# Dealing the next group's dots between the stages on VectorE, with gelu behind ScalarE's stages

## The reference, cut to what matters

```
h  = rmsnorm(x) @ w_in                        # latents, rotary keys, conv inputs
o  = softmax(q_lat.ckv + q_rope.kr) ckv       # 4 heads, causal; the 8 samples read paged caches of 2048 keys
x1 = x + [group_rmsnorm(attn), group_rmsnorm(conv)] @ w_o
q  = rmsnorm(x1) @ w_query                    # 8 heads x 2 x 128
sv, si = top_k(q . sub_keys, 16)              # per half
experts, g = top 16 of the 16 x 16 sums, softmax of their scores     # 8 x 16 = 128 slots a token
a  = gelu(x . expert_u[experts])
x2 = x1 + sum over the 128 slots of (g * a) * expert_v[experts]
y  = rmsnorm(x2)
```

## Time and profile before

| what | value |
|---|---|
| median of 3 runs | 3510.18 us (3496.6 to 3515.45) |
| the profiled execution | 3510.76 us, its span 3509.0 us |
| busy share of the span | PE 72%, DVE 65%, POOL 66%, ACT 23% |
| mean granted clock of TensorE | 0.839 of full speed |
| moved by DMA | 1279.45 MB |
| its queues' share of 16 engines | gathers (POOL's) 80.6%, SP's 12.5%, ACT's 2.3% |

### The profile page before, as it was taken

One profiled execution on the slowest core, in us unless ns is written; L12 is line 12 of the kernel. 1 busy time (PEld: TensorE's weight loads), 2 busy tenths in 40 slices (PEclk: granted clock), 3 DMA queues, 4 the chain that ended last, 5 costly groups with the idle time before them and its releaser, 6 DMA issues.

```text
span 3509.0 us, 38717 instructions
## 1 busy us (share of the span) xinstructions
PE 2510.7 (72%) x11488; PEld 1386.8 (40%) x11488; DVE 2278.5 (65%) x5454; ACT 813.6 (23%) x2057; POOL 2300.2 (66%) x2068
## 2 busy tenths in 40 slices
PE   7558775878764598877644977778546888875755
PEld 6426443545531264445311643345213534332421
DVE  3685586655688756657898466558796454544874
ACT  2112212232212212322112123322113122222111
POOL 0466575755657777676777767667777585657774
PEclk9779887999986799898876999889777798988776
DMA  6699899988999999999999999899999999999997
GB/s 237 241 389 375 329 410 333 392 306 302 372 346 373 373 402 372 353 369 412 408 359 375 405 385 355 329 376 409 400 368 374 379 388 359 371 334 398 411 409 305
DMA packets 368935, 1279.45 MB, mean 365 GB/s; under 512 B 59372, under 2 KB 77974, under 8 KB 353368
## 3 DMA queue, kind: packets, MB, share of 16 engines
q0 software_dynamic: 297216, 1082.26, 80.6%
q1 hardware_dynamic: 62324, 168.67, 12.5%
q10 hardware_dynamic: 9188, 26.05, 2.3%
HBM read 1262.31 MB, written 13.48 MB: 364 GB/s over the span
## 4 chain that ended last, share of the span: by engine, by line
DVE 37%; PE 31%; DMA 15%; issue 7%; ACT 4%; SPq 3%; POOL 2%; DVEq 0%; ACTq 0%; POOLq 0%
DVE u_ring L1736 15%; PE acc L924 9%; DMA u_ring<-in_expert_u,pick_cur 8%; PE front L586 8%; PE front L802 3%; DMA v_ring<-in_expert_v,pick_cur 3%; DVE si_u L1603 2%; SPq L536 2%; DVE sv L1602 2%; PE front L711 2%; DMA w_ukT<-in_cache_krope 2%; DVE work L1603 2%; DVE work L1602 1%; DVE work L1647 1%; DVE work L1649 1%
## 5 line engine op out<-in xcount | busy, mean ns | idle before, releaser
L924 PE MATMUL acc<-v_ring,diag 128*64 128x512 f32 x4096 | 1176.0, 723 | 614.6 <-ACT diag L1222 344.4
L1851 POOL DMA_INDIRECT v_ring<-in_expert_v,pick_cur x1024 | 1146.5, 1120 | 607.3 <-PE acc L924 334.3
L1851 POOL DMA_INDIRECT u_ring<-in_expert_u,pick_cur x1024 | 1136.9, 1110 | 569.1 <-issue 292.3
L1736 DVE CUSTOM_DVE_ANT_0 u_ring<-u_ring,xn_cur 128x1024 f32<-128x1024 f32 x1024 | 1209.9, 1222 | 335.1 <-DMA u_ring<-in_expert_u,pick_cur 329.4
L924 PEld LDWEIGHTS acc<-v_ring,diag 128*64 128x64 f32 x4096 | 342.6, 164 | 1331.4 <-issue 878.5
L1222 ACT ACTIVATE diag<-ident,wgt 128x64 f32<-128x64 f32 x1024 | 272.8, 338 | 787.1 <-DVE wgt L1742 734.9
L586 PE MATMUL front<-work,w_ring 128*128 128x256 f32 (+2 forms) x1536 | 306.4, 341 | 31.8 <-DVE mo L1337 17.1
L586 PE MATMUL front<-mo,w_ring 128*128 128x256 f32 (+2 forms) x1536 | 298.2, 335 | 0.0
L1215 ACT ACTIVATE gelu<-dots 128x4 f32<-128x4 f32 x256 | 52.7, 206 | 996.5 <-DVE dots L1736 992.8
L586 PEld LDWEIGHTS front<-work,w_ring 128*128 128x128 f32 x1536 | 249.0, 199 | 83.9 <-issue 28.6
L586 PEld LDWEIGHTS front<-mo,w_ring 128*128 128x128 f32 x1536 | 252.0, 198 | 23.9
(11 more groups left out here) (303 smaller groups left out, 2375.7 us busy)
## 6 DMA issues: line engine op xcount, KB each, us to landing
w_ring<-in_w_pieces SPq DMA_DIRECT2D x112, 1024.0 KB, 8.4
u_ring<-in_expert_u,pick_cur POOLq DMA_INDIRECT x1024, 10.5
v_ring<-in_expert_v,pick_cur POOLq DMA_INDIRECT x1024, 9.9
x_t<-in_x_prompt SPq DMA_DIRECT2D x16, 512.0 KB
v_ring<-in_w_pieces SPq DMA_DIRECT2D x8, 1024.0 KB, 12.0
work<-in_cache_ckv SPq DMA_DIRECT2D x64, 128.0 KB, 15.2
xn_cur<-scratch ACTq DMA_DIRECT2D x14, 512.0 KB, 9.7
scratch_x<-rows_next ACTq DMA_DIRECT2D x8, 512.0 KB, 6.8
```

The costliest lines, as they stand in the source:

```text
L924: last = nc.tensor.matmul(acc[rows, half, :], diag[:, s % RING, :], v_ring[:, s % RING, half * 512:half * 512 + 512], start=(s < 2), stop= ...
L1736: v.tensor_tensor_reduce(u_ring[:, slot, :], u_ring[:, slot, :], xn2_cur[:, block_of(r), :], 1.0, 0.0, ALU.mult, ALU.add, dots[:, g * G + ...
L1851: pool.indirect_dma_start(ring[:, slot, :], None, a[table][0], bass.IndirectOffsetOnAxis(ap=pick, axis=0)).then_inc(loaded[slot], 16)
```

## The change

On DVE the dots of g+1 are cut in shares: one share stands at the head of the group, ahead of the weighing of g, and one behind each stage. With no stage or one the shares are 2 and 2; with two stages 2, 1, 1; with three 1, 1, 1, 1. On ACT gelu of g+1 (and the load of the next tile's tokens) always stands behind the stages. PE, POOL and SP keep their order, and the special cases for `pages` go.

```diff
+def shares(n, k):
+    cuts = [(n * i + k) // (k + 1) for i in range(k + 2)]
+    return list(zip(cuts[:-1], cuts[1:]))
...
             def tile(it):                                   # ScalarE
                 for g, stages in enumerate(PLAN[it]):
-                    late = has_pages(stages)
                     if g:
                         diag_group(it, g)
-                    if g and not late and g + 1 < GROUPS:
-                        gelu_group(it, g + 1)
-                    if g == GROUPS - 2 and not late and it < LAST:
-                        load_xn2(it + 1)
                     for s in stages:
                         stage(own, *s)
-                    if g and late and g + 1 < GROUPS:
+                    if g and g + 1 < GROUPS:
                         gelu_group(it, g + 1)
-                    if g == GROUPS - 2 and late and it < LAST:
+                    if g == GROUPS - 2 and it < LAST:
                         load_xn2(it + 1)
...
             def tile(it):                                   # VectorE
                 for g, stages in enumerate(PLAN[it]):
-                    half = G // 2 if has_pages(stages) else G
+                    dots_due = g > 0 and g + 1 < GROUPS
+                    parts = shares(G, max(1, len(stages)))
+                    if dots_due:
+                        dot_group(it, g + 1, *parts[0])
                     if g:
                         weigh_group(it, g)
-                    if g and g + 1 < GROUPS:
-                        dot_group(it, g + 1, 0, half)
-                    ahead = 1 if has_pages(stages) else len(stages)
-                    for s in stages[:ahead]:
-                        stage(own, *s)
-                    if g and g + 1 < GROUPS:
-                        dot_group(it, g + 1, half, G)
-                    for s in stages[ahead:]:
-                        stage(own, *s)
+                    for n, part in enumerate(parts[1:]):
+                        if n < len(stages):
+                            stage(own, *stages[n])
+                        if dots_due:
+                            dot_group(it, g + 1, *part)
```

## The result

The changed kernel takes 3563.82 us (median of 5, 3561.53 to 3565.84) against 3503.06 us (median of 5, 3496.6 to 3515.45): ratio 1.0162, 95% interval 1.0146 to 1.0179, so slower by 57 us (the two medians lie 61 us apart). The profiled execution took 3563.91 us, its span 3562.1 us at a mean clock of 0.843; before it was 0.839, so the clock is no part of the loss. The forecast was 3531 us: its sign holds, its size is a third of the loss.

The account below looks back on a forecast made before the run. No single engine bounds the program; it alternates. Terms +13 +10 +5 +8 -10 -5 +4 -5 sum to +20 us on 3510.8: forecast 3531 us, own range 3518 to 3555, whole range 3482 to 3580.

Parts of the forecast that it names:

- Term 1: One-stage query groups: MAX8 waits for the scores' copy behind ACT's diags, 0.87 us more each; +13 us, ends 0 and +21.
- Term 2: Groups without stages behind a long DVE stage: a late weigh holds PE's v_group; +10 us, and +5 behind a `select`.
- Term 3: Selects and long stages: POOL stops at the third u gather; ends 0 and 126 us, taken +8 at three tops stretches.
- Term 4: Multi-stage groups: a dot fills each DVE wait between stages; ends 0 and -26 us, taken -10.
- Term 5: gelu behind ACT's stages: weigh's wait for it goes under dots, -5 us; Exp and Ln tables load behind diag, +4.
- A: Rival, whole kernel: the DMA sets the pace, no change; 3505 to 3518 us, say 3512; chance 0.30.
- B: Rival, multi-stage groups: faster, all 23 holes pay; -32 us, 3479 us; chance 0.24.
- C: Rival: clearly slower, POOL stands at the third u through every select and long stage; 3565, at worst about 3600 us; chance 0.12.

Follow-up runs that it names:

- e14: The changed kernel with the weighing ahead of the dots only in the 40 groups whose one stage is a query: 1.0081 of the kernel before.
- e7: The changed kernel with ACT copying the scores ahead of the diags in groups that begin with a query: 1.0176 of the kernel before, second occasion.
- e1: The kernel before with the ACT part of the change alone, gelu behind ACT's stages, DVE's order as before: 0.9978 of the kernel before.
- e10: The changed kernel with the weighing ahead of the dots only in the 29 groups without a stage: 1.0168 of the kernel before.
- e11: The changed kernel with the weighing ahead only in groups whose one stage is no query: 1.0136 of the kernel before.
- e6b: The changed kernel with POOL's order fitted to the dot shares in tiles 1 to 5 alone, fourth occasion: 1.0164 of the kernel before.
- e13: The changed kernel with the weighing ahead of the first share and POOL's order fitted in tiles 1 to 5: 1.0013 of the kernel before.
- e3b: The changed kernel with the weighing ahead of the first share in all groups, fourth occasion: 1.0021 of the kernel before.
- e6: The changed kernel with POOL's order fitted to the dot shares in tiles 1 to 5 alone, second occasion: 1.0157 of the kernel before.
- e9: The kernel before with gelu behind ACT's stages and the scores' copy ahead of the diags, VectorE as before: 0.9935 of the kernel before.
- e4: The kernel before with the changed order only in groups with two or three stages: 1.0013 of the kernel before.
- e12: Same as e9, with dots dealt out in groups of two and three stages behind a weighing that stays ahead: 0.9921 of the kernel before.
- e0: The changed kernel unedited, run again on the second occasion as the mark: 1.0251 of the kernel before.
- e5: The kernel before with only the weighing moved behind the four dots: 1.0256 of the kernel before, second occasion.

## Why the forecast was right in sign and wrong in size

The change is slower for the reason that the forecast gave first, a weighing that comes too late. Two steps failed. The late weighing (terms 1 and 2) was taken at +28 us, and putting it ahead gives 49. And the load of the next tile's tokens, which the change moves with gelu and which waits for the tile's last dots, had no term at all: the tile ends where it is waited for cost 26 us.

**Term 1 (MAX8 behind the diags): right.** Its 0.87 us per group is 0.85 in the row (0.60 to 1.45). The one-stage query groups add 20 us in sum, against +13 taken and an end of +21. Leaving nine groups out, because they run into waits for u rows, was the error in it: tiles 3, 5 and 7 give 13.5 of the 20, and tiles 0 and 1 only 6.6. In tile 1 the weighings of two neighbouring query groups lie 12.42 us apart before (mean of that tile) and 13.29 now, 0.87 more. e14 and e7 show the path. What the forecast had not seen is that the ACT part alone *removes* part of the 0.60 us, since gelu no longer waits for the last dot ahead of the copy: the MAX8 line waits 52.6 us in e1 and 57.1 in e14, against 77.3 in the kernel before. The late weighing takes this gain away too, which fits that moving it forward gives 28 us and not 13 to 21.

**Term 2 (a late weigh holds PE's v_group): the mechanism stands, its place and price failed.** Behind mix_norm, in the changed kernel, DVE and PE:

```profile
1527.29 1.23 DVE L1569 TENSOR_TENSOR work<-work,vec_cols 128x1024 f32<-128x1024 f32 x1
```
```profile
1532.89 5.54 PE L930 MATMUL acc<-v_ring,diag 128*64 128x512 f32 x16 [10.80 <-ACT diag L1228]
```

From the start of mix_norm's last operation to the v_group it is 5.60 us. Before, that operation, which stood just ahead of the earlier trace rows, was

```profile
1518.88 1.23 DVE L1568 TENSOR_TENSOR work<-work,vec_cols 128x1024 f32<-128x1024 f32 x1
```

and the v_group followed at 1521.05, 2.17 us behind. The 3.43 us are the forecast's 3.44. But e10, which puts the weighing back in all 29 groups without a stage, shortens that stretch:

```profile
1531.82 1.23 DVE L1569 TENSOR_TENSOR work<-work,vec_cols 128x1024 f32<-128x1024 f32 x1
...
1534.46 0.16 DVE L1743 TENSOR_TENSOR wgt<-gelu,gate_cur 128x4 f32<-128x4 f32 x1 [0.27 <-ACT gelu L1221]
```
```profile
1535.49 5.10 PE L930 MATMUL acc<-v_ring,diag 128*64 128x512 f32 x16 [10.01 <-ACT diag L1228]
```

to 3.67 us, and shows no gain: 1.0168. The +10 and +5 were worth 0, with some 8 us either way left open by the intervals. Meanwhile the forecast gave nothing to one-stage groups other than queries: by the stage matching they lose 13 us, and e11 has 0.26%, 9 us, there, which its interval does not tell from nothing. The weighing ahead everywhere gives 49 us (1.0162 to 1.0021); with 28 in query groups, 9 in other one-stage groups and 0 without a stage, each within some 10 us, some 12 us are left to groups of several stages or to what only shows when all are moved. Terms 1 and 2 together had +28.

**Term 3 (POOL meets a closed door): it costs nothing where it was read, and beside it a term is missing, the tokens' load.** "It costs nothing if the queues hold enough ... and all of it if POOL is full afterwards", and then I took the near end, +8 us at three tops stretches. At the select that I had read it costs nothing, indeed. POOL stops at the third u gather, as forecast, but its idle there is what it was ahead of the first one in the earlier trace rows:

```profile
1112.52 1.18 POOL L1851 DMA_INDIRECT u_ring<-in_expert_u,pick_cur  x1 [5.04 <-DVE dots L1737]
```

With POOL's order fitted nothing comes back on the fourth occasion (e6b, and e13 beside e3b), 0.9% on the second (e6). The cost that no part of the sum holds is at the tile ends, 26 us by the jumps above. The forecast puts ACT's load of the next tile's tokens at nothing by not naming it, though the change moves it. It takes 12.7 to 13.7 us from issue to landing, and at all six ends the first dot starts 0.02 to 0.12 us behind the landing.

The jumps stay in every kernel that splits the dots around a single stage (e3b 24 us, e13 25 us). e9 moves the load behind ACT's stages but has all four dots ahead of them: its jumps are 8 us, and its dots still wait for the tokens in tiles 0, 2 and 4 (7.06, 2.30 and 12.47 us). So some 8 us belong to ACT's order and the rest, 18, to the late share. Over e1, where the kernel before was at its longer level, e4 has -3, e12 3, e0 10 and e6 17 us, but e5 has 11 without any late share, so there something else adds to them. No kernel moved the load by itself, and what an earlier one would give back was not measured.

**Term 4 (a dot in each hole): right where it was read, nothing in sum.** Between two heads of tile 1 the dot stands where the wait for the transposes was the earlier trace rows:

```profile
727.47 0.61 DVE L1494 SCALAR_TENSOR_TENSOR work<-low_keys,small,front 128x384 f32<-128x384 f32 x1 [1.16 <-PE front L718]
...
733.61 0.16 DVE L1743 TENSOR_TENSOR wgt<-gelu,gate_cur 128x4 f32<-128x4 f32 x1
...
735.20 0.61 DVE L1494 SCALAR_TENSOR_TENSOR work<-low_keys,small,front 128x384 f32<-128x384 f32 x1 [0.97 <-PE front L718]
```

The 0.64 us is gone and 1.57 became 1.16; in exchange a wait of 0.97 us for the scores stands behind the front dots. The group has 12.84 us from weighing to weighing (720.77 to 733.61), before 13.39 (721.66 to 735.05): 0.5 us shorter, where the chain of front, PE and v_group was to give near nothing. In tile 1, behind its norms, after lies 9 us before the old kernel, and 5.5 us ahead of its tops; over the whole program the groups of several stages, without the tile ends, come out at -5 us against the -10 taken, and e4, which deals out in these alone, at 1.0013.

**Term 5 (gelu): right on its wait.** Weigh waits for gelu 16 times instead of 80, 22.3 us instead of 33.2. Of these, 8 (6.7 us) stand in the last group of a tile; the longest, 6.4 us, is in tile 1 (weighing at 705.8), where gelu now stands behind ACT's part of three stages. gelu's table is still loaded 80 times and hides. e1's 0.9978 agrees with -5 + 4 within its interval; what it is worth beyond the MAX8 waits was not measured.

**The sum again, by place**, in the two profiled executions (+53 us): query stages +20 (forecast 13), tile ends +26 (no term; the 8 of term 3 stood at the tops), other one-stage groups +13 and groups of several stages -5 (together with the rest +7, forecast -1 without the 8). And by cause, in medians: late weighing +49 (forecast 28); late shares and the rest +7 (forecast -8), in which tile ends of some 25 us (still there in e3b) and the gains elsewhere stand against each other.

**The rivals.** A (the DMA sets the pace) held in part in tile 0, where the DMA is near its limit: the MAX8 waits of its query groups grow by 8.8 us and their stages end 3.5 us later. B's holes pay little. C asked for idle of over 10 us ahead of that u gather; it is 5.04, so C did not happen though the time is near its 3565: the right number by another sum.

## What to carry to other kernels

When operations are rotated in a loop, look first at the small one: a weighing of 0.16 us, moved behind 2.3 us of dots, cost 1.4% of the program, over half of it (0.81%) in the groups where a copy on another engine was queued behind four operations that wait for it. Put what other engines wait for first and the bulk behind it, and let an engine that copies for a waiting one do this copy ahead of work that nobody needs yet (e9: 0.65% in five runs with an interval of 0.4%, gelu's move included). When the last readers of a buffer with one copy move back, the load that refills it moves back too: here DVE's idle time at six tile ends grew with it from 15 to 43 us. A stage by stage difference of two traces shows where time goes when no total of waits does: here POOL's wait for dots grew by 287 us in a kernel that takes 1.0021 of the time (e3b).

## What the runs showed that I had not expected

- The same edit cost 1.6% on one occasion and 2.5% on another. It is not the chip alone: on chip 13 the kernel before took 3609, 3607 and then 3505 us. With e0 at 1.0251 POOL's fitted order was worth 0.9% (e6 1.0157, intervals that touch), with the changed kernel at 1.0162 nothing (1.0164). What takes longer stays open: e0's dots take 1.22 us each and its MAX8 0.29, as in the changed kernel's trace, and through the query stretch of tile 0 (450 to 550 us) e1's DMA moved 410 GB/s, as much as in the earlier trace rows.
- A gather that starts after a wait for DVE costs POOL 1.18 us instead of 0.94, and one behind it up to 1.99 in the rows of this case, while DVE runs dots; how much of POOL's 66% busy time that is was not tried.
